# The gate and value products of a second feed-forward expansion by Strassen's scheme (Winograd's form), with its sums on the vector engine and the low halves shared by two engines

## What is computed

```python
def swiglu(h, w_in, w_out):            # h: 512 x 1024, w_in: 1024 x 5632, w_out: 2816 x 1024
    a, b = jnp.split(h @ w_in, 2, axis=-1)
    return (jax.nn.silu(a) * b) @ w_out

h = rmsnorm(x, ffn_norm_pre[i]) * (1.0 + sc2) + sh2
y = swiglu(h, ffn_w_in[i], ffn_w_out[i])
x = x + g2 * rmsnorm(y, ffn_norm_post[i])
```

## Time and profile before

| | |
|---|---|
| time, median of 3 runs (lowest, highest) | 1345.88 us (1344.02, 1346.18) |
| span of the profiled execution | 1343.4 us; its own time is not listed apart, and the median is 2.5 us above this span |
| PE busy | 1295.9 us, 96% of the span |
| POOL busy | 591.2 us, 44% |
| ACT busy | 568.5 us, 42% |
| DVE busy | 544.9 us, 41% |
| mean granted TensorE clock | 0.984 of full speed |
| weights: 92 loads of 1 MB | 4.7 us each from issue to landing |

### The profile page before, as it was taken

The page is one execution under the profiler, slowest core; times in us unless marked ns, Lnnn a source line. Parts: engine busy times, 40 slices in busy tenths (PEclk is TensorE's granted clock), DMA queues, the critical chain, the costliest instruction groups (busy, mean ns, idle before and its releaser), DMA issues.

```text
span 1343.4 us, 17523 instructions
## 1 busy us (share of the span) xinstructions
PE 1295.9 (96%) x6464; PEld 1042.2 (78%) x6464; DVE 544.9 (41%) x1080; ACT 568.5 (42%) x938; POOL 591.2 (44%) x494
## 2 busy tenths in 40 slices
PE   7899999998989999999999899999899999999998
PEld 1688878677878888888888788667688888888886
DVE  2576652678436444443542352783520000001113
ACT  3713455767344322233323454785452323223232
POOL 0334332468043444444665733455224444445561
PEclk9999999999889999999999999899999999999999
DMA  9427557050243555554423411111202222222221
GB/s 393 179 77 270 187 172 142 1 189 1 73 178 125 199 200 196 187 187 157 157 94 99 162 64 69 56 30 61 91 32 97 98 105 105 95 94 94 94 94 63
DMA packets 27402, 166.77 MB, mean 124 GB/s; under 512 B 2976, under 2 KB 5280, under 8 KB 8656
## 3 DMA queue, kind: packets, MB, share of 16 engines
q1 hardware_dynamic: 25328, 151.31, 32.4%
q10 hardware_dynamic: 2016, 14.68, 2.9%
HBM read 163.85 MB, written 6.32 MB: 127 GB/s over the span
## 4 chain that ended last, share of the span: by engine, by line
PE 85%; DVE 6%; ACT 3%; DMA 3%; issue 1%; POOL 1%; SPq 0%; DVEq 0%; ACTq 0%
PE bank L275 55%; PE bank L334 12%; PE bank L311 6%; DMA ada_ring<-ada_dram 2%; DVE ada_ring L2018 1%; PE bank L1357 1%; PE bank L1329 1%; PE bank L714 1%; DMA w_raw<-w_dram 1%; PE bank L523 1%; DVE arena L2083 1%; PE bank L537 1%; PE bank L509 1%; PE bank L690 1%; POOL arena L942 1%
## 5 line engine op out<-in xcount | busy, mean ns | idle before, releaser
L268 POOL TENSOR_TENSOR w_lo<-w_raw,w_hi 128x512 fp32r<-128x512 f32 x328 | 444.0, 1385 | 620.2 <-ACT w_hi L259 620.2
L275 PE MATMUL bank<-h_hi,w_hi 128*128 128x512 f32 x1088 | 429.6, 395 | 7.4 <-DVE h_lo L450 4.5
L275 PE MATMUL bank<-h_lo,w_hi 128*128 128x512 f32 x1088 | 426.8, 392 | 0.0
L275 PE MATMUL bank<-h_hi,w_lo 128*128 128x512 f32 x1088 | 426.8, 392 | 0.0
L259 ACT ACTIVATE w_hi<-w_raw 128x2048 fp32r<-128x2048 f32 x86 | 164.8, 1917 | 309.0 <-PE bank L275 190.3
L275 PEld LDWEIGHTS bank<-h_hi,w_hi 128*128 128x128 f32 x1088 | 206.0, 189 | 51.4 <-issue 7.9
L275 PEld LDWEIGHTS bank<-h_hi,w_lo 128*128 128x128 f32 x1088 | 206.2, 190 | 43.5
L275 PEld LDWEIGHTS bank<-h_lo,w_hi 128*128 128x128 f32 x1088 | 206.4, 190 | 41.3
L2355 DVE TENSOR_TENSOR arena<-arena,bank 128x512 f32 (+1 forms) x22 | 15.1, 688 | 210.2 <-PE bank L275 210.2
L2211 DVE TENSOR_TENSOR h_lo<-arena,h_hi 128x1024 fp32r<-128x1024 f32 x22 | 32.4, 1485 | 135.1 <-ACT h_hi L1832 123.6
L2037 DVE SCALAR_TENSOR_TENSOR arena<-bank,params,arena 128x511 f32<-128x511 f32 (+1 forms) x36 | 25.3, 704 | 131.9 <-ACT arena L1807 111.6
(11 more groups left out here) (278 smaller groups left out, 1783.9 us busy)
## 6 DMA issues: line engine op xcount, KB each, us to landing
w_raw<-w_dram SPq DMA_DIRECT2D x92, 1024.0 KB, 4.7
ada_ring<-ada_dram SPq DMA_DIRECT2D x30, 1024.0 KB, 4.8
ada_ring<-ada_dram ACTq DMA_DIRECT2D x14, 1024.0 KB, 4.8
arena<-ada_dram SPq DMA_DIRECT2D x4, 1024.0 KB, 10.7
arena<-x_dram SPq DMA_DIRECT2D x2, 2048.0 KB, 11.5
bias_copies<-bias_rows SPq DMA_DIRECT2D x1, 4096.0 KB, 17.2
arena<-bias_copies SPq DMA_DIRECT2D x4, 768.0 KB, 5.7
ada_ring<-rpb_dram SPq DMA_DIRECT2D x16, 128.0 KB, 9.7
```

Of the source, the lines that this page charges most:

```text
L268: last = nc.gpsimd.tensor_tensor(w_lo[b % 2][:, part], w_raw[b % 2][:, part], w_hi[b % 2][:, part], ALU.subtract)
L275: last = nc.tensor.matmul(bank[:, :], w[:, ft, k, :], x[:, k, :], start=k == first and m == 0, stop=k == final and m == 2)
```

## The change

```diff
+            def seven(n, i=0):
+                pe.wait_ge(tile_free, F_UP2 + 2 * n + 2 + 4 * i)
+                for p in range(7):
+                    if p in (3, 4):
+                        pe.wait_ge(seven_low, 2 + 2 * n + p - 2 + 4 * i)
+                    else:
+                        pe.wait_ge(lo_done, LOW0 + 5 * n + (p + 1 if p < 3 else p - 1) + 10 * i)
...
+                    if p == 4:
+                        pe.wait_ge(seven_snap, 2 * n + 1 + 4 * i)
+                    if p in (5, 6):
+                        pe.wait_ge(seven_sum, 4 * n + (2 if p == 5 else 1) + 8 * i)
...
+                    for k in range(4):
+                        for m, (w, x) in enumerate(((hi, x_hi), (hi, x_lo), (lo, x_hi))):
+                            last = nc.tensor.matmul(out, w[:, k], x[:, k], start=k == 0 and m == 0, stop=k == 3 and m == 2)
+                    last.then_inc(half_used, 1)
...
-            tiles(B_UP2 + 2, F_UP2 + 4, 9)
-            last_turn(B_UP2 + 20, F_UP2 + 40)
+            seven(0)
+            seven(1)
+            with pe.Fori(0, 9) as i:
+                seven(2, i)
+                seven(3, i)
...
+            def pool_turn(n, i=0):
+                for p in (0, 1, 2):
+                    low_slot(n + 1, p, i)
+                for p in (5, 6):
+                    low_slot(n + 1, p, i)
+            low_slot(0, 0)
+            low_slot(0, 1)
+            low_turned(2)
+            low_turned(0)
+            for p in (2, 5, 6):
+                low_slot(0, p)
...
+            def act_turn(n, i=0):
+                for p in range(7):
+                    if p == 0:
+                        snapshot(n, p, p1_copy, i)
+                    if p == 4:
+                        snapshot(n, p, p5_copy, i)
+                    if p == 6:
+                        gate_silu(n, i)
+                    high_slot(n + 1, p, i)
...
+            def dve_turn(n, i=0):
+                if n:
+                    left_value(n - 1, i)
+                weight_sums(n + 1, i)
+                if n == 0:
+                    plain_gated(1)
+                else:
+                    gated2(n - 1, i)
+                weight_sums_too(n + 1, i)
+                left_gate(n, i)
+                third_sum(n, i)
+                low_slot(n + 1, 3, i)
+                more_sums(n, i)
+                low_slot(n + 1, 4, i)
+                right_gate(n, i)
...
             def down_rows(b0, g0, bank_free):
+                pe.wait_ge(tile_free, bank_free - 2)
                 pe.wait_ge(g_split, g0 + 1)
-                pe.wait_ge(lo_done, b0 + 1)
+                pe.wait_ge(lo_done, low_after(b0))
```

More of the change, by code:

```diff
@@ L418, in spread, with affine @@
             return last
-        def affine(act, m, gain, shift, xn, hb, aside=None, turned=None):
+        def affine(act, m, gain, shift, xn, hb, aside=None, turned=None, slots=2):
             for c in range(DC):
@@ L1660, in whole @@
                     pe.wait_ge(g_split, g0 + t + 1 + off)
[L1661 removed]
+                    pe.wait_ge(lo_done, low_after(b0 + t) + off)
                     w = row_weights(b0 + t)
@@ new lines, in snapshot, with gate_silu @@
+            def snapshot(n, p, copy, i=0):
+                act.wait_ge(half_used, USED0 + 7 * n + p + 1 + 14 * i)
+                nc.scalar.activation(copy[n % 2], product_at(n, p), ACT.Copy).then_inc(seven_snap, 1)
+            def gate_silu(n, i=0):
+                act.wait_ge(seven_sum, 4 * n + 3 + 8 * i)
+                nc.scalar.activation(gate_sum[n % 2], gate_sum[n % 2], ACT.Silu).then_inc(tap_silu, 1)
+            def act_turn(n, i=0):
[7 more added lines that the diff above has]
+                    high_slot(n + 1, p, i)
@@ new lines, in plain_silu @@
+            def plain_silu(u):
+                act.wait_ge(half_used, 2 * B_UP2 + 2 * u + 1)
+                nc.scalar.activation(gate_sum[u], ps[2 * u][:, :], ACT.Silu).then_inc(tap_silu, 1)
+            high_slot(0, 0)
+            for k, t in enumerate(TURNED):
+                act.wait_ge(t_sum, max(k, t) + 1)
+                nc.scalar.activation(t_parts[t][0], h_sums[:, t], ACT.Copy).then_inc(t_high, 1)
+            plain_silu(0)
+            for p in (1, 2, 3):
+                high_slot(0, p)
@@ new lines, in _ @@
+            plain_silu(1)
+            for p in (4, 5, 6):
+                high_slot(0, p)
+            with act.Fori(0, 9) as i:
+                act_turn(0, i)
+                act_turn(1, i)
+            act_turn(18)
+            snapshot(19, 0, p1_copy)
+            for t in range(2):
+                nc.scalar.activation(h_hi[:, 2 * t:2 * t + 2, :], HID[:, 2 * t:2 * t + 2, :], ACT.Copy).then_inc(g_hi, 1)
+            act.wait_ge(half_used, USED0 + 7 * 19 + 4)
+            act.wait_ge(raw_in[1], 16 * (B_DOWN2 // 2 + 1))
@@ L1987, in _ @@
+            nc.scalar.activation(w_hi[1][:], w_raw[1][:], ACT.Copy).then_inc(hi_done, 1)
+            snapshot(19, 4, p5_copy)
+            gate_silu(19)
+            high(act, B_DOWN2 + 1)
             act.wait_ge(tile_free, F_UP2 + 44)
@@ new lines, in left_value, with gated2 @@
+            def left_value(n, i=0):
+                dve.wait_ge(half_used, USED0 + 7 * n + 7 + 14 * i)
+                nc.vector.tensor_tensor(value_sum[n % 2][:, 0:256], product_at(n, 6), u3[n % 2], ALU.add).then_inc(seven_sum, 1)
+            def gated2(n, i=0):
+                dve.wait_ge(tap_silu, 36 + n + 3 + 2 * i)
+                dve.wait_ge(seven_more, 2 * n + 2 + 4 * i)
+                dve.wait_ge(seven_sum, 4 * n + 4 + 8 * i)
+                nc.vector.tensor_tensor(HID[:, bass.ds(n + 2 + 2 * i, 1), :].rearrange("p a n -> p (a n)"), gate_sum[n % 2], value_sum[n % 2],
+                                        ALU.mult).then_inc(tile_free, 2)
@@ L2362, in _ @@
+            dve_turn(18)
+            left_value(18)
+            gated2(18)
             hidden_low(12, slice(0, 2), 0)
+            left_gate(19)
+            third_sum(19)
             hidden_low(13, slice(2, 4), 2)
-            gated2(21)
+            more_sums(19)
+            right_gate(19)
+            left_value(19)
+            gated2(19)
             with dve.Fori(0, 3) as i:
```

215 lines of the change are left out of this document (166 added, 49 removed).

## The result

| | before | after |
|---|---|---|
| time, median (lowest, highest) | 1345.81 us (1344.02, 1346.18), 4 runs | 1401.18 us (1399.55, 1401.96), 4 runs |
| span of the profiled execution | 1343.4 us | 1400.2 us |
| mean granted TensorE clock | 0.984 | 0.963 |

The ratio is 1.0416, with a 95% interval of 1.0401 to 1.0430: **55.4 us slower**. The forecast was 1386 us, 40 more, with a range of 1358 to 1416.

A forecast was written before the change was run, and what follows sets the result against it. PE alone was taken to bound the stage before; afterwards DVE and POOL taking turns would hold it up. 16.2 + 18 x 12.65 + 9.83 + 3.7 = 257.4 us replaces 217.2: 40 us more, 1386 us, range 1358 to 1416.

The forecast's parts named there:

- The mechanism: Second expansion: DVE instructions with two SBUF operands and POOL's low halves shut each other out, delaying `third_sum`; PE stands 2.8 us.
- PE's work: Second expansion: 84 matmuls at 0.117 us make 9.83 us a block against 10.86, 20.6 us saved over 20 blocks.
- What a turn costs: DVE beside POOL: a 512-column instruction with two SBUF operands holds POOL up 0.50 us, beside POOL's own 1.25.
- The block, at full clock: Each block of the second expansion: 9.83 us of matmuls plus 2.8 us standing ahead of product 5, 12.65 us.
- The clock: PE in the second expansion: the sum took no cost for a lower granted clock and left it to a rival.
- Rival 3: PE's gap in each block lowers the clock: 1.7 us a block, up to 34 us more, 1420 us; 15%.
- in a half of the blocks: The lower clock follows PE's gap in only half of the expansion's blocks: 1403 us.
- The main case: Whole kernel: 1375 to 1398 us, from hand-offs of 0.05 more or less and 0.46 or 0.53 held; 62%.
- Three turns and not four: Three POOL instructions between `left_value` and `third_sum`: 11.4 us a block, 1362 us as a rival; 13%.
- Start and end: First block 16.2 us, standing 3.4 ahead of product 2 and 2.9 ahead of product 5; 3.7 us standing at the end.
- Rival 4: Whole kernel: losses and gain cancel at 10.7 us a block, time within 0.2% of before; 2%.
- Rival 1: PE stays the bound in the expansion: 9.83 us a block, 15 us faster, 1331 us; 8%.

The follow-up runs named there:

- the filler: Changed kernel with 16 unread 128x256 matmuls more in each block, between PE's waits for slot 5 and for `third_sum`; 1376.6 us, ratio 1.0236.
- the last kernel: The one before it, with DVE's order of the change restored (SUM3 and SUM4 ahead of `left_gate` and `third_sum`); 1338.14 us, ratio 0.9956.
- the one before it: Changed kernel with `third_sum` moved up, SUM1, SUM3 and Silu written to PSUM, `more_sums` reading product 4 there, POOL's turned halves earlier; 1326.12 us, ratio 0.9875.

## Why the prediction came out as it did

**The mechanism: right.** DVE's sums at 1.6 to 1.7 us, POOL's at 1.5 to 1.7, `left_gate` at 0.68, PE idle once a block ahead of product 5 for `third_sum`: the marks that the prediction set are in the rows, POOL's a little below the 1.75 it named. Cutting POOL short removes all of it, and moving `third_sum` or the operands removes most.

**PE's work: right.** 0.117 us a matmul; 9.83 us were predicted for a block and 9.76 measured where nothing holds it. The 262 cycles of the Trainium skill, "TensorE: Matmul & The Clock Gate", section "Back-to-back issue gap", an estimated 9.2 us a block, would have been too low.

**What a turn costs: near.** Turns are 1.70 us, so a 512-column instruction of DVE costs POOL 0.45; 0.50 was predicted. By the Trainium skill, "SBUF — State Buffer", section "SBUF: two separate sides", the shared ports are held for the full instruction, which makes a turn 1.25 + 0.69 = 1.94 us, an estimate. On how long they are held the rows disagree with the page.

**The block, at full clock: 0.4 us too long.** 12.65 was predicted and 12.25 measured with the filler. A turn is 1.70 us and not 1.75 (0.2 over four); `left_value` starts 0.20 behind the turn of the block and not 0.34; the hand-off from DVE to PE is 0.05 and not 0.1. Over 18 blocks that is 7 us too much. The three parts together are the 0.4 us.

**The clock: the step that failed.** Rival 3 was the truth, at 15%, and its cost was kept out of the sum, which put the clock at nothing. The argument against it was that dense matmuls lie on both sides of the gap, whereas ahead of the expansion several gaps followed one another. The rows refute it: a single gap of some 2.2 us amid dense matmuls was followed by the lower clock in 17 of 18 blocks. Its price was right, 1.7 us each. Its time, 1420, was not reached: the block it was added to was too long (7 us over 18 blocks), there were 17 falls in the loop and not 20 (5 us), and each gave some 0.25 us back (4 us). That 1403, the same rival "in a half of the blocks", lies so near the 1401 measured is luck; the falls came in nearly all blocks. The main case, 1375 to 1398, was missed. The range held because it took in most of the clock's cost.

**Three turns and not four: near as a price, in one block.** The block from 1084.1 us takes 11.01 us (11.4 predicted); 0.3 of it is the end of the lower clock of the block before. There `gated2` starts 0.03 us before POOL's next instruction and gets through in 0.68:

```profile
1087.01 0.68 DVE L2574 TENSOR_TENSOR arena<-ada_ring 128x512 f32 x1
1087.62 1.79 DVE L2531 TENSOR_TENSOR arena<-w_raw 128x512 f32<-128x512 f32 x1
```

```profile
1087.04 1.81 POOL L1377 TENSOR_TENSOR w_lo<-w_raw,w_hi 128x512 fp32r<-128x512 f32 x1 [0.50 <-ACT w_hi L2106]
```

POOL still has four instructions there, but the last of them runs mostly beside `left_gate`, which reads PSUM and is not held up. One turn less, PE stands 0.8 us, and there is no fall of the clock: here the two costs go together.

**Start and end.** In the first block PE stood 2.9 us ahead of product 2 (3.4 predicted) and only 0.9 ahead of product 5, for POOL's low half of slot 5 and not for `third_sum` (2.9 predicted); a fall of the clock, some 1.6 us, stood in no sum. That these make 15.47 us where 16.2 were predicted is partly luck. Ahead of the reduction PE goes 3.7 us from one start to the next, as predicted.

**The account.** Predicted 16.2 + 227.7 + 9.83 + 3.7 = 257.4; measured 15.5 + 243.2 + 9.7 + 3.7 = 272.0. The 18 blocks of the loop are 15.5 us longer than predicted, the two ends 0.9 shorter. The clock adds 17 x 1.7 = +28.9. PE stands 2.2 us where 2.82 were predicted: 17 x 0.62 = -10.5, in which is the 0.25 us that the slower clock gives back. 84 matmuls take 9.76 and not 9.83: -1.3. The one short block is -1.6. Together +15.5.

**Sums that do not come out.** Rival 4's block of 10.7 us gives 1351 us by the prediction's own start and end; the losses cancel at 10.4. Rival 1 takes 1.5 us for the start where the sum has 3.4. No row shows the 0.53 us of the main case's bounds. None of these changes the forecast.

## What to carry to other kernels

When work goes to an engine that is "only half busy", check which of its instructions read two SBUF operands while GpSimd works, and what waits behind them: DVE's work, 7.0 us a block where POOL was cut short, fitted easily beside PE's 9.8, but in turns with POOL the result that PE waited for came 9.1 us after the block's start, where PE was free at 7. Put what the matrix engine waits for ahead of what nobody waits for, and let an operand lie in PSUM where a bank is free; here either one took back 42 to 54 of the 55 us lost. And where a forecast has PE stand 2 us in each turn of a loop, put the lower clock into the sum, not among the rivals: 1.7 us for each fall here, 1.4 net, in 17 of 18 blocks.

## What the runs showed that was not expected

- **A gap of about 2.2 us in each block brought the lower clock with it, one of 1.3 did not.** Falls by standing time ahead of product 5: 2.1 to 2.8 us in the changed kernel's loop, 17 of 17; 0.8 us (its short block), none; 1.3 us (`third_sum` moved), none in the loop; 0.6 to 0.7 us, none; 1.7 us (the last block with `third_sum` moved), none; 2.4 us filled with unread matmuls up to the last 0.5 us, none. Between 1.7 and 2.1 us nothing was tried.
- **The length of a gap alone does not settle it.** The wait of 2.8 us ahead of product 2 of the first block was followed by a fall in the changed kernel and in three of its variants, but not in the trace with the filler, where that wait is as long and unfilled: in the 3.40 us behind it 16 matmuls started at 0.51 of the clock in the one, 29 at 1.00 in the other. The wait of 3.1 us ahead of the reduction went with a fall in the last kernel and with none in the one before it. What else decides was not tested.
- **Unread matmuls pay.** 16 of them a block, in a wait, gave 24.6 us. In the last block of the twenty there was no such wait, and their 1.9 us vanished in PE's wait ahead of the reduction.
- **A result in PSUM frees nothing:** SUM3 with its output there and both reads in SBUF took 1.79 us, as with its output in SBUF.
- **Hundredths can decide who goes first.** `gated2` took 0.68 us and not 1.78 in the block where it started 0.03 us ahead of POOL's instruction, and that block is 2.6 us shorter. It is one block, read and not tested.
